# Four of eight sample-state stores moved behind the last one, with six ada groups one or two steps earlier

## The reference, cut to what matters

```python
z = h @ w_in                                   # q, k, v, r, a_lr, u
S_new = exp(b_end) * S + k^T v                 # one state per sample: 4 heads x 128 x 256
o = (q * exp(b)) @ S + ...                     # each sample's query reads its state
new_gla_sample = S_new                         # an output, 512 KB per sample
d = window_sum(u) / count - u                  # pooling windows 2, 4, 8, 16
y_pool = (d @ pool_w) * pool_scale
mod = silu(c) @ w_ada + b_ada                  # shift, scale, gate: six blocks of 2048 columns
```

## Time and profile before

| what | value |
|---|---|
| median of 3 runs (lowest, highest) | 2540.3 us (2539.91, 2542.41) |
| the profiled execution | 2540.4 us |
| its span | 2538.6 us |
| mean granted TensorE clock | 0.996 |
| PE busy | 2498.6 us, 98% |
| DVE, ACT, POOL busy | 1509.9, 985.5, 157.5 us |
| chain of waits: PE, DMA, DVE, ACT | 92%, 3%, 2%, 2% |
| DMA | 620.50 MB, mean 244 GB/s |

### The profile page before, as it was taken

One profiled execution on the slowest core, in us unless ns is written; L12 is line 12 of the kernel. 1 busy time (PEld: TensorE's weight loads), 2 busy tenths in 40 slices (PEclk: granted clock), 3 DMA queues, 4 the chain that ended last, 5 costly groups with the idle time before them and its releaser, 6 DMA issues.

```text
span 2538.6 us, 59285 instructions
## 1 busy us (share of the span) xinstructions
PE 2498.6 (98%) x24993; PEld 2420.8 (95%) x24993; DVE 1509.9 (59%) x2265; ACT 985.5 (39%) x1144; POOL 157.5 (6%) x211
## 2 busy tenths in 40 slices
PE   7999999999999999999999999999999999999998
PEld 6888799999999999999999999999999999999998
DVE  4575555554454455445548999996755654654654
ACT  3243343332333332333335565656433333333333
POOL 1000331000000000000020020300000000000011
PEclk9999999999999999999999999999999999999999
DMA  9999989899999998998655474745555555555553
GB/s 351 371 353 323 325 303 311 274 311 313 302 311 304 307 309 299 307 307 296 221 182 176 156 245 159 254 153 167 172 178 181 182 179 174 178 181 182 177 175 130
DMA packets 475913, 620.50 MB, mean 244 GB/s; under 512 B 10871, under 2 KB 375829, under 8 KB 471641
## 3 DMA queue, kind: packets, MB, share of 16 engines
q1 hardware_dynamic: 467682, 591.70, 70.2%
q0 software_dynamic: 8096, 26.84, 3.1%
HBM read 606.62 MB, written 13.29 MB: 244 GB/s over the span
## 4 chain that ended last, share of the span: by engine, by line
PE 92%; DMA 3%; DVE 2%; ACT 2%; issue 1%; SPq 0%; ACTq 0%; DVEq 0%
PE ps L1013 26%; PE ps L1014 26%; PE ps L1015 26%; PE pm L1140 5%; PE ps L1057 2%; DMA wide<-in_w_ada 2%; DMA raw<-in_ev_w_in 1%; PE pm L1122 1%; PE ps L1221 1%; PE ps L1222 1%; PE ps L1223 1%; DVE w_lo L2284 1%; PE pm L1160 1%; PE pm L1342 1%; ACT w_hi L1712 1%
## 5 line engine op out<-in xcount | busy, mean ns | idle before, releaser
L2284 DVE TENSOR_TENSOR w_lo<-raw,w_hi 128x1024 fp32r<-128x1024 f32 x700 | 867.4, 1241 | 840.1 <-ACT w_hi L1712 833.6
L1712 ACT ACTIVATE w_hi<-raw 128x1024 fp32r<-128x1024 f32 x688 | 726.8, 1058 | 1208.7 <-PE ps L1015 1179.1
L1013 PE MATMUL ps<-h_hi,w_hi 128*128 128x264 f32 x3552 | 1025.2, 289 | 4.5 <-issue 1.6
L1014 PE MATMUL ps<-h_lo,w_hi 128*128 128x264 f32 x3552 | 1013.0, 285 | 0.0
L1015 PE MATMUL ps<-h_hi,w_lo 128*128 128x264 f32 x3552 | 1011.2, 285 | 0.0
L1013 PEld LDWEIGHTS ps<-h_hi,w_hi 128*128 128x128 f32 x3552 | 671.0, 189 | 18.0 <-issue 13.0
L1014 PEld LDWEIGHTS ps<-h_lo,w_hi 128*128 128x128 f32 x3552 | 669.2, 188 | 1.5 <-issue 0.8
L1015 PEld LDWEIGHTS ps<-h_hi,w_lo 128*128 128x128 f32 x3552 | 669.5, 188 | 0.0
L1013 PE MATMUL ps<-f_hi,w_hi 128*128 128x264 f32 x2048 | 584.2, 285 | 0.0
L1014 PE MATMUL ps<-f_lo,w_hi 128*128 128x264 f32 x2048 | 584.2, 285 | 0.0
L1015 PE MATMUL ps<-f_hi,w_lo 128*128 128x264 f32 x2048 | 583.1, 285 | 0.0
(11 more groups left out here) (423 smaller groups left out, 1669.8 us busy)
## 6 DMA issues: line engine op xcount, KB each, us to landing
raw<-in_mlp_w_up SPq DMA_DIRECT2D x128, 1024.0 KB, 5.9
raw<-in_mlp_w_down SPq DMA_DIRECT2D x128, 1024.0 KB, 5.3
wide<-in_w_ada SPq DMA_DIRECT2D x104, 1024.0 KB, 8.9
wide_late<-in_w_ada SPq DMA_DIRECT2D x56, 1024.0 KB, 9.3
raw<-in_od_w_in SPq DMA_DIRECT2D x48, 1024.0 KB, 5.2
raw<-in_ev_w_in SPq DMA_DIRECT2D x32, 1024.0 KB, 10.0
araw<-in_w_ada SPq DMA_DIRECT2D x24, 1024.0 KB, 8.9
raw<-in_ev_w_out SPq DMA_DIRECT2D x16, 1024.0 KB, 6.0
```

Of the source, the lines that this page charges most:

```text
L1013: nc.tensor.matmul(acc, w_hi[:, slot, cols], xh[:, k, :], start=(k == UK * ends[0]), stop=False)
L1014: nc.tensor.matmul(acc, w_hi[:, slot, cols], xl[:, k, :], start=False, stop=False)
L1712: nc.scalar.activation(w_hi[:, u, :], raw[:, p, u, :], ACT.Copy).then_inc(hi_ready, 1)
L2284: nc.vector.tensor_tensor(w_lo[:, p, u, :], raw[:, p, u, :], w_hi[:, u, :].bitcast(F32), ALU.subtract).then_inc(lo_ready, 1)
```

## The change

The stores of states 3, 4, 5 and 6 of layer 0 (counted from 0) are issued by POOL after that of state 7, and no longer each after its own update. POOL's wait before `pool_w` is now for the stores of states 1 and 7 alone, and that for states 2 to 6 stands before the window sums. DVE's wait for the stores moves from ahead of the reductions of the past (L2802) to ahead of the instructions that write `z` (L2808). Six ada groups move: g8 to g13 (`RATES_AT` counts them from 0) go from steps 17, 20, 23, 26, 30, 33 to 15, 18, 22, 25, 29, 32. The order of SP's queue stays.

```diff
-RATES_AT = dict(zip((0, 1, 2, 4, 6, 8, 10, 12, 17, 20, 23, 26, 30, 33, 36, 39), range(16)))
+RATES_AT = dict(zip((0, 1, 2, 4, 6, 8, 10, 12, 15, 18, 22, 25, 29, 32, 36, 39), range(16)))
+LATE_STORES = (3, 4, 5, 6)
...
                 for b in range(NS):
                     pool.wait_ge(st_ready, NS * q + b + 1)
-                    pool.dma_start(dst[b, hsl].rearrange("h k v -> k h v"),
-                                   state(q, b).rearrange("p (h v) -> p h v", h=HG)).then_inc(st_out[b % nb], 16)
+                    if q or b not in LATE_STORES:
+                        store(b)
...
+                if q == 0:
+                    for b in LATE_STORES:
+                        store(b)
...
-            for b in range(NS - HEADS[0]["bufs"], NS):
+            for b in (1, NS - 1):
                 pool.wait_ge(st_out[b % HEADS[0]["bufs"]], 16 * transfers(0, b))
             pool.wait_ge(o8_psum, NS)
             pool.dma_start(pool_w[:, :, :, :], ...).then_inc(aw_in, 16)
             pool.wait_ge(evacuated, 12)
-            pool.wait_ge(o8_psum, NS)
+            for b in range(2, NS - 1):
+                pool.wait_ge(st_out[b], 16 * transfers(0, b))
...
                 dve.wait_ge(evacuated, 12)
-                for b in range(NS - HEADS[0]["bufs"], NS):
-                    dve.wait_ge(st_out[b % HEADS[0]["bufs"]], 16 * transfers(0, b))
...
                 step(nc.vector.tensor_tensor(t8[:, 0:8, :], t8[:, 0:8, :], z[:, 24:32, TP:T], ALU.add))
+                for b in range(NS - HEADS[0]["bufs"], NS):
+                    dve.wait_ge(st_out[b % HEADS[0]["bufs"]], 16 * transfers(0, b))
```

More of the change, by code:

```diff
@@ L893, in states, with store @@
                 yield
+                def store(b):
+                    pool.dma_start(dst[b, hsl].rearrange("h k v -> k h v"),
+                                   state(q, b).rearrange("p (h v) -> p h v", h=HG)).then_inc(st_out[b % nb], 16)
                 for b in range(NS):
                     pool.wait_ge(st_ready, NS * q + b + 1)
-                    pool.dma_start(dst[b, hsl].rearrange("h k v -> k h v"),
-                                   state(q, b).rearrange("p (h v) -> p h v", h=HG)).then_inc(st_out[b % nb], 16)
+                    if q or b not in LATE_STORES:
+                        store(b)
                     if b < nb - at_once:
```

## The result

The changed kernel takes 2556.0 us (median of 6 runs, 2554.7 to 2558.5) against 2539.8 us for the one before (6 runs): 0.64% slower, ratio 1.0064 with the interval 1.0051 to 1.0077. That it would be slower was forecast, by how much was not: the forecast was 2549.2 us, and the result lies 2 us above its range, 2540 to 2554. The profiled execution took 2558.5 us, 18.1 us more than the profiled one of before.

What follows compares the result with a forecast made beforehand. PE was taken as the bound, busy for 98% of the span and 92% of the chain of waits. -4.2 + 5.8 + 5.0 + 0 + 0.7 + 1.5 = +8.8 us on 2540.4 gave 2549.2 us, range 2540 to 2554.

Steps and rivals of the forecast that it cites:

- Part 1: Step 30: with four stores later, w14a is in time and the DMA stall goes; 4.2 us gained, bounds 4.2 and 6.3.
- Part 2: Step 18: g9 waits for r9, queued behind w11b; 5.8 us lost, bounds 1.4 and 7.3.
- (a): Rival: loads quicker in their new places, step 18 costs 3.6 us and step 25 2.5 us; 2542.3 us, chance 0.20.
- Part 3: Step 25: g11 waits for r11, asked for right behind w13a; 5.0 us lost, bounds 4.0 and 6.5.
- Part 4: Steps 29 and 32: g12 and g13 cost nothing; 0, bounds 0 and 1.5 us.
- Part 5: Window sums start later behind the late stores, beyond their 7.7 us of cover; 0.7 us lost, bounds 0 and 3.
- Clock: Behind the two new waits, steps 18 and 25: a lower PE clock can cost 1.5 us each; one counted.
- (b): Rival: neither ada group waits, only the stall's removal counts, 4.2 to 6.3 us; 2535 us, chance 0.05.
- (c): Rival: late stores also harm; r13 1.5 us late, window sums 3 us, clock falls twice; 2554.5 us, chance 0.13.

Runs made afterwards that it cites:

- e2: The kernel before with only the ada groups moved to the change's steps, all stores in their old places: 2556.5 us, ratio 1.0067.
- e1: The changed kernel with the ada groups back in their old steps, so only the stores are late: 2543.6 us, ratio 1.0015.
- e7: e3 with the stores of states 1 and 2 late as well: 2552.4 us (one run).
- e8: e3 with g10 back in step 23 too, g11 still in step 25: 2546.6 us (one run).
- e3: The changed kernel with g9 back in step 20, all else as it is: 2548.5 us, ratio 1.0032.
- e4: The changed kernel with SP's queue reordered, r9 ahead of w11b and r11 ahead of w13a: 2539.2 us, ratio 0.9997.
- e5: The kernel before with e4's queue order and g8 to g11 in steps 15, 18, 22, 25; all stores in place: 2538.2 us, ratio 0.9990.
- e11: The changed kernel with g9 back in step 20 and g11 in step 26, SP's queue as it is: 2544.5 us, ratio 1.0015.
- e6: e5 with the stores of states 5 and 6 alone issued behind store 7: 2536.7 us, ratio 0.9987.
- e9: e6 with the load of pastu issued ahead of the first store instead of behind the sixth: 2534.9 us, ratio 0.9981.

## Why the prediction was right in its direction and wrong in its size

**Part 1, the stall of step 30.** w14a was in time, but that is partly luck: e2 has it in time with every store in place, since PE came some 17 us later there, and in e1, where PE does not, the four stores brought it 3.9 us sooner and not 5.4, 0.4 us too late. Right that PE would wait for the chain behind unit 52's split, now uncovered: 2.1 us forecast, 2.2 measured. Wrong in the next term: I gave unit 53 the full clock. It ran at 0.50 for most of its length, and 2.4 us were gained, not 4.2. In e2, e7 and e8, where the clock stayed, the same count gives 3.9 us.

**Part 2, step 18.** Right in place, cause and wait: halves at 239.1 and 242.4 forecast, 239.2 and 241.7 measured; idle 3.57 + 1.39 = 5.0 us against 5.8. e3 takes it out alone, e4 shows that it hangs on the queue's order. The step cost 8.1 us because 3.1 us of lower clock came with it. The lower bound, 1.4 us, is a slip: from 230.75, with 1.84 us to the second request, 4.8 to its landing and 0.93 for its work, it is 0.8. Only rival (a) uses it.

**Part 3, step 25.** Right in place and cause, too small in the wait. I held r11's landing to 14.7 us after unit 45's end; it was 17.2. I had moved g10 ahead of unit 45 and kept POOL's stores where they were against that unit, though they follow unit 44; so the first of them and a state's load came ahead of r11. e7 and e8 bear that out. The idle time was 7.0 us, less the 0.46 of before 6.6, in place of 5.0; and the lower clock cost another 4.3 us: 10.9 us.

**Part 4.** Right: g12 and g13 wait for nothing.

**Part 5, the sums.** 0.7 us forecast, 1.5 measured. Its real weight shows in e1, where PE is not delayed ahead of it.

**Clock.** This is the step that failed: "either can cost 1.5 us. I count one." Both waits brought the lower clock, so did the 2.2 us at step 30, which I had not counted at all, and each cost more than the case I took the 1.5 us from: 3.1, 4.3 and 1.8 us, 9.2 us in place of 1.5. My other terms sum to -4.2 + 5.8 + 5.0 + 0.7 = 7.3 us. The errors of the idle times add -0.8 + 1.6 + 0.8 = 1.6 us, the clock 9.2: 18.1 us, the difference of the profiled executions. The range's upper end, 2554, had two drops of 1.5 us in it and none at step 30. The 9.2 us are those of one execution: the lower clock of step 25 cost 3.2 us in e3 and 5.3 in e7, that of step 18 1.8 us in e2, and step 30 had none in e2, e7 and e8. So a part of the size is chance.

**The rivals.** (a) and (b) needed quicker ada halves; e4 shows that an earlier request would have made them so, and the change has none. (c) came nearest, 2554.5 us, and not for all its reasons: r13 was not late, the sums cost 1.5 us and not 3, and the clock fell three times and not twice, at 1.8 to 4.3 us each in place of 1.5.

## What to carry to other kernels

Before an operation is moved earlier, read when its load is requested: if the request stands behind another one in a queue whose order stays, the operation waits, whatever bandwidth was freed (e4: two pairs of requests moved, 17 us back). A transfer taken off one place comes down in another; ask who waits for its end there, and with how much cover once the stall is gone (e1). Count an idle stretch of PE of 2.2 us or more, as those here, with what may follow it at half clock, here up to 5 us, and put a drop that may or may not come into the range.

## What the runs showed of the hardware

- Behind single idle stretches of PE of 2.2 to 2.3 us the granted clock fell to 0.50 in six cases (the wait for the copy in the changed kernel, e3, e4, e5 and e11, the first wait for the sums in e1) and stayed at 1.00 in three (the wait for the copy in e2, e7 and e8). It fell with every one of 3.5 us and more, in e2, e3 and e7 (step 25) while PE was still idle, and stayed with those of 1.2 to 1.5 us (the copy in e6, the sums in the changed kernel and e9).
- After a wait in two parts (5.2 and 1.8 us, step 25 of the changed kernel, with half a group at the lower clock between them) the clock was at 0.50 from 285 to 294 us, through the second part and for some 6 us behind it.
- 1 MB of stores on POOL's queue beside 2 MB of loads on SP's delayed the loads by 1.4 us (e3 against e7, one profile each).
- An instruction of POOL (L956, in the kernel before L946 with 0.25 us) took 1.12 us in six runs and ended 0.1 us after DVE's split in the two compared above.
